# Neighbourhood attention: two pairs of score banks, one bank each for the results and the turned pieces

## The chip, the cores and the metric

One core of a Trainium2 chip runs the whole program. The metric is device time in microseconds, the median of three runs.

## The reference

Two transformer blocks over 1024 tokens of width 1024, in fp32. The change lies in one part of the first block, the neighbourhood attention: 16 heads of width 32, on a grid of 16 rows by 64 columns. A query sees the 8 grid rows around its own (`WIN_R`) and 16 columns (`WIN_C`):

```python
sc = jnp.einsum('bjqhd,bjkhd->bhjqk', qb, kg).astype(jnp.float32) * scale + bias
pr = jax.nn.softmax(sc, axis=-1).astype(vg.dtype)
o = jnp.einsum('bhjqk,bjkhd->bjqhd', pr, vg)
```

## The kernel before, in words

`neighbourhood_phase` (L2385) takes the 16 heads as four quads of four, and in each quad the 16 grid rows: 64 steps g. A step works on one grid row, 64 queries by 4 heads, against 8 rows of keys (512). It goes through these pieces of work, each a small function written once for its engine, with semaphores between them and the order written out by hand:

- `score` (PE, L2458): six matmuls in three passes (q and k are split into a high and a low part) into `psS`, two banks of 512.
- `add_bias` (DVE, L2584): for each of the two banks one instruction that adds the bias and keeps the running minimum of the negated scores. It takes no semaphore of its own, so the waits stand on the instruction before it: `clear_spare` (L2592), a memset of one column of a spare tile, or, from g = 2 on, the reciprocal in `out_of`.
- `exps` (ACT, L2553): the exponentials, one instruction for each of the two banks.
- `turn_e` (PE, L2486): eight transposes of the exponentials into `psT` (banks 4 and 5). `take` (ACT, L2562) copies them out.
- `multiply` (PE, L2496): 16 small matmuls with v into `psO` and 16 with ones into `psR`, the row sums.
- `out_of` (DVE, L2596): reciprocal of the sums, then the product into `att_T`.

Beside this, the next quad's q and k are brought into shape during the current quad: eight pieces (four of k, then four of q), one per step from r = 4 (`TURN_AT`) to r = 11. `turn` (PE, L2474) transposes a piece, `take_high` (ACT, L2540) rounds it to the high part a step later, and `take_low` (DVE, L2607) subtracts to the low part and so sets the bank free (`lowered`). The first quad's eight pieces are turned ahead of the loop.

PE's order in step g (L2527 to L2535) is turn_e(g), score(g+2), multiply(g-1), then a piece where there is one. ACT's (L2571 to L2577) is exps(g+1), take(g), then the high part of a piece. DVE's (L2636 to L2650):

```python
if g + 2 < STEPS:
    dve.wait_ge(scored, g + 3)
    dve.wait_ge(exped, 2 * g + 2)
...
if g >= 2:
    out_of(g - 2)
if g + 2 < STEPS:
    add_bias(g + 2)
if q + 1 < QUADS and 0 <= r - TURN_AT - 1 < PIECES:
    take_low(q + 1, r - TURN_AT - 1)
```

The eight banks of PSUM before: 0 and 1 the scores (one pair, so score(g) waits at L2463 until add_bias(g-1) is done), 2 and 3 the turned pieces by turns (a piece waits at L2481 for the one two back), 4 and 5 the turned exponentials, 6 and 7 results and sums by turns (multiply waits at L2501 for the out_of two back). SP loads q, k, bias and v a quad ahead (L2436 to L2448), each behind a wait on the quad that used the buffer. POOL sets the ones and does nothing else in the loop.

Of the kernel before, what the change touches and what calls it, by code (L numbers as in the profile page):

```python
# [2384 lines left out]
def neighbourhood_phase(nc, k, proj, att, after):  # L2385
    Q0, K0, V0 = 3 * 512, 4 * 512, 5 * 512
    QC = 4 * DB_H
    with ExitStack() as stack:
# [14 lines left out]
        inv_T = s.sb("inv_T", [P, GRID])  # L2403
        own = s.sb("own", [P, 2])
        neg_max = [[s.sb(f"neg_max{a}{b}", [P, 1]) for b in range(2)] for a in range(2)]
        spare = s.sb("spare", [P, 4])
        psS = [k.ps[:, b, :] for b in range(2)]
        psT = k.ps[:, 4:6, :].rearrange("p b n -> p (b n)")
        psO, psR = ([k.ps[:, 6 + a, i * GRID:(i + 1) * GRID] for a in range(2)] for i in range(2))
        psP = [k.ps[:, 2 + a, 0:PC] for a in range(2)]  # L2410

        loaded, v_loaded, bias_loaded = s.sems("loaded", 2), s.sems("v_loaded", 2), s.sems("bias_loaded", 2)
        spared, lowered, own_set, turned, taken = (s.sem(n) for n in ("spared", "lowered", "own_set", "turned", "taken"))
# [42 lines left out]
        @block.tensor  # L2456
        def _(pe):
            def score(g):  # L2458

                q, r = divmod(g, ROWS)  # L2460
                a = r % 2
                if g >= 1:
                    pe.wait_ge(biased, 2 * g)  # L2463
                if r == 0:
                    pe.wait_ge(lowered, PIECES * (q + 1))
                for i_pass, (qq, kk) in enumerate(((q_hi, k_hi), (q_lo, k_hi), (q_hi, k_lo))):
                    for b in range(2):
                        two = slice(b * 2 * DB_H, (b + 1) * 2 * DB_H)
                        last = pe.matmul(psS[b], qq[q % 2][two, r, :, :].rearrange("p h c -> p (h c)"),
                                         kk[q % 2][two, first_row(r) * GRID:first_row(r) * GRID + CH],  # L2470
                                         start=(i_pass == 0), stop=(i_pass == 2))
                last.then_inc(scored, 1)

            def turn(q, j):  # L2474
                i, m = 1 - j // (PIECES // 2), j % (PIECES // 2)
                if m == 0 and isinstance(q, int) and q == 0:
                    pe.wait_ge(k.na_loaded[i], 16)
                elif m == 0:
                    pe.wait_ge(loaded[i], 16 * q)
                if PIECES * q + j > 1:  # L2480
                    pe.wait_ge(lowered, PIECES * q + j - 1)  # L2481
                for n in range(2):
                    last = pe.transpose(psP[j % 2][:, n * P:(n + 1) * P], raw[i][:, 2 * m + n, :], k.ident[:])
                last.then_inc(turned, 1)

            def turn_e(g):  # L2486

                pe.wait_ge(exped, 2 * g + 2)
                if g >= 1:
                    pe.wait_ge(eT_ready, g)  # L2490
                for b in range(2):
                    for n in range(4):
                        last = pe.transpose(psT[:, b * CH + n * P:b * CH + (n + 1) * P], e[g % 2][b][:, n * P:(n + 1) * P], k.ident[:])
                last.then_inc(e_turned, 1)

            def multiply(g):  # L2496

                q, r = divmod(g, ROWS)
                a = r % 2
                if g >= 2:  # L2500
                    pe.wait_ge(row_out, g - 1)  # L2501
                if r == 0:
                    pe.wait_ge(v_loaded[q % 2], 32 * (q // 2 + 1))
                pe.wait_ge(eT_ready, g + 1)

                def weights(h, n):
                    at = h // 2 * CH + n * P + h % 2 * GRID
                    return eT[a][:, at:at + GRID]

                for n in range(4):  # L2510
                    row = first_row(r) + 2 * n
                    vv = (v_even if row % 2 == 0 else v_odd)[q % 2]
                    for h in range(4):
                        part = slice(h * DB_H, (h + 1) * DB_H)
                        pe.matmul(psO[a][part, :], vv[:, row // 2, part], weights(h, n), start=(n == 0), stop=(n == 3))
                for n in range(4):
                    for h in range(4):
                        part = slice(h * DB_H, (h + 1) * DB_H)
                        last = pe.matmul(psR[a][part, :], ones[:], weights(h, n), start=(n == 0), stop=(n == 3))
                last.then_inc(multiplied, 1)  # L2520

            for j in range(PIECES):
                turn(0, j)
            score(0)
            score(1)
            pe.wait_ge(ones_set, 1)
            for g in range(STEPS):  # L2527
                q, r = divmod(g, ROWS)
                turn_e(g)
                if g + 2 < STEPS:  # L2530
                    score(g + 2)
                if g >= 1:
                    multiply(g - 1)
                if q + 1 < QUADS and 0 <= r - TURN_AT < PIECES:
                    turn(q + 1, r - TURN_AT)  # L2535
            multiply(STEPS - 1)

        @block.scalar
        def _(act):
            def take_high(q, j):  # L2540
                i, m = 1 - j // (PIECES // 2), j % (PIECES // 2)
                act.wait_ge(turned, PIECES * q + j + 1)
                if i == 0 and q == 0 and m == 0:
                    act.wait_ge(own_set, 8)
                if i == 1:
                    act.copy(k_hi[q % 2][:, m * PC:(m + 1) * PC], psP[j % 2]).then_inc(taken, 1)
                    return
                for slot in range(2):
                    last = act.activation(q_hi[q % 2][:, m * PR:(m + 1) * PR, slot, :], psP[j % 2].rearrange("p (r c) -> p r c", c=GRID),
                                          ACT.Copy, scale=own[:, slot:slot + 1])  # L2550
                last.then_inc(taken, 1)

# [27 lines left out]
        def _(dve):  # L2580
# [3 lines left out]
            def add_bias(g):  # L2584

                a, off_g = g % 2, off(g % ROWS)
                for b in range(2):
                    nb = bias[g // ROWS % 2][:, b, off_g:off_g + WIN_R, :].rearrange("p r c -> p (r c)")
                    dve.tensor_tensor_reduce(sc[a][b][:], psS[b], nb, 1.0, BIG, ALU.add, ALU.min,  # L2589
                                             neg_max[a][b][:]).then_inc(biased, 1)  # L2590

            def clear_spare(col):  # L2592

                dve.memset(spare[:, col:col + 1], 0.0).then_inc(spared, 1)

            def out_of(g):  # L2596

                q, r = divmod(g, ROWS)
                dve.wait_ge(multiplied, g + 1)
                if g > 0:  # L2600
                    dve.wait_ge(row_out, g)
                dve.reciprocal(inv_T[:], psR[g % 2]).then_inc(inverted, 1)
                dve.wait_ge(inverted, g + 1)
                dve.tensor_tensor(k.att_T[:, q, r * GRID:(r + 1) * GRID], psO[g % 2], inv_T[:],
                                  ALU.mult).then_inc(row_out, 1)

            def take_low(q, j):  # L2607
                i, m = 1 - j // (PIECES // 2), j % (PIECES // 2)
                dve.wait_ge(taken, PIECES * q + j + 1)
                if i == 0 and q == 0 and m == 0:  # L2610
                    dve.wait_ge(own_set, 8)
                if i == 1:
                    cols = slice(m * PC, (m + 1) * PC)
                    dve.tensor_tensor(k_lo[q % 2][:, cols], psP[j % 2], k_hi[q % 2][:, cols].bitcast(F), ALU.subtract).then_inc(lowered, 1)
                    return
                for slot in range(2):
                    rows = slice(m * PR, (m + 1) * PR)
                    last = dve.scalar_tensor_tensor(out=q_lo[q % 2][:, rows, slot, :], in0=psP[j % 2].rearrange("p (r c) -> p r c", c=GRID),
                                                    scalar=own[:, slot:slot + 1], in1=q_hi[q % 2][:, rows, slot, :].bitcast(F),
                                                    op0=ALU.mult, op1=ALU.subtract)  # L2620
                last.then_inc(lowered, 1)
# [13 lines left out]
            add_bias(1)  # L2635
            for g in range(STEPS):  # L2636
                q, r = divmod(g, ROWS)
                if g + 2 < STEPS:
                    dve.wait_ge(scored, g + 3)
                    dve.wait_ge(exped, 2 * g + 2)  # L2640
                    if r == ROWS - 2:
                        dve.wait_ge(bias_loaded[(q + 1) % 2], 16 * ((q + 1) // 2 + 1))
                if g < 2:
                    clear_spare(2 + g)
                if g >= 2:
                    out_of(g - 2)
                if g + 2 < STEPS:
                    add_bias(g + 2)
                if q + 1 < QUADS and 0 <= r - TURN_AT - 1 < PIECES:
                    take_low(q + 1, r - TURN_AT - 1)  # L2650
# [702 lines left out]
```

## Time and profile before

| what | value |
|---|---|
| median of three runs | 3104.11 us (3103.66 to 3104.99) |
| the profiled execution | 3107.22 us |
| its span, first to last instruction | 3105.5 us |
| PE busy, weight loads busy | 2787.9 us (90%), 2190.9 us (71%) |
| DVE, ACT, POOL busy | 1740.6 (56%), 1239.4 (40%), 298.6 us (10%) |
| mean granted clock of TensorE | 0.949 of full speed |

The shares are of the whole span, and stages with other limits stand side by side in them. PE is TensorE's matmuls, PEld its weight loads, DVE VectorE, ACT ScalarE, POOL GpSimd, SP the engine that issues most transfers. A granted clock of 1.00 is 2.4 GHz, 0.50 is 1.2 GHz. Profiled executions have a time of their own, a little above the median of the runs.

### The profile page before, as it was taken

How to read it: one execution, taken by the hardware profiler on the slowest of the kernel's cores; microseconds unless marked ns; L12 is line 12 of the kernel's file. 1: busy time of each engine (PE TensorE's matmuls, PEld its weight loads, DVE VectorE, ACT ScalarE, POOL GpSimd, SP SyncE). 2: the span in 40 equal slices, each digit the busy share in tenths (PEclk: the TensorE clock that was granted, in tenths of full speed). 3: DMA queues.
4: the chain of work that ended last, by engine and by line, in shares of the span. 5: the costliest groups of instructions: out<-in, count | busy, mean ns of one | idle time of the engine just before them, and what ended most of it. 6: DMA issues, size and time to landing. Idle time of an engine off the chain costs nothing. (4 is left out here: it accounts for less than half of the span.)

```text
span 3105.5 us, 60538 instructions
## 1 busy us (share of the span) xinstructions
PE 2787.9 (90%) x24014; PEld 2190.9 (71%) x24014; DVE 1740.6 (56%) x3213; ACT 1239.4 (40%) x2039; POOL 298.6 (10%) x459
## 2 busy tenths in 40 slices
PE   7999896999869999999788999978888999968888
PEld 6787664777648877777576888765567888865557
DVE  4762777676151222222265677469865667559874
ACT  4332564785041010000065322258842332249861
POOL 0000562000031222222100000000000000000000
PEclk9999998999989999999899999989889999989989
DMA  5222755212369999999864233351035223270024
GB/s 181 91 78 76 235 164 157 76 49 78 115 263 323 374 380 380 377 374 378 286 239 152 68 109 109 123 165 28 1 123 173 78 84 110 78 219 28 14 82 142
DMA packets 226424, 509.35 MB, mean 164 GB/s; under 512 B 29217, under 2 KB 101729, under 8 KB 201537
## 3 DMA queue, kind: packets, MB, share of 16 engines
q1 hardware_dynamic: 202448, 448.57, 40.4%
q0 software_dynamic: 22640, 58.01, 6.9%
q8 instruction: 122, 2.00, 0.3%
q14 instruction: 62, 0.50, 0.1%
q10 hardware_dynamic: 1152, 0.27, 0.0%
HBM read 414.04 MB, written 93.66 MB: 163 GB/s over the span
## 5 line engine op out<-in xcount | busy, mean ns | idle before, releaser
L1933 PE MATMUL ps<-w_up,ex_xT 128*32 128x384 f32 x3072 | 343.8, 489 | 17.9 <-DMA w_up<-in_w_dram 17.0
L1935 PE MATMUL ps<-w_up,ex_xT 128*32 128x128 f32 x3072 | 348.0, 274 | 0.0
L1935 PEld LDWEIGHTS ps<-w_up,ex_xT 128*32 128x32 f32 x3072 | 331.3, 110 | 0.4
L1884 DVE TENSOR_TENSOR ex_hid<-ps,ex_act 32x128 f32<-32x128 f32 x96 | 28.2, 294 | 303.4 <-PE ps L1935 302.6
L927 ACT CAST next_w<-early 128x512 fp32r<-128x512 f32 x128 | 79.7, 622 | 256.6 <-PE ps L1245 219.4
L1960 PE MATMUL ps<-w_down,ex_hT 128*32 128x512 f32 (+1 forms) x1536 | 173.4, 491 | 6.8 <-DMA w_down<-in_w_dram 6.0
L1962 PE MATMUL ps<-w_down,ex_hT 128*32 128x256 f32 x768 | 173.6, 383 | 0.0
L1029 DVE TENSOR_TENSOR next_w<-early,next_w 128x512 fp32r<-128x512 f32 x128 | 88.2, 690 | 134.8 <-ACT next_w L927 133.9
L694 PE MATMUL ps<-mix_in_wh,mix_in_xh 128*128 128x512 f32 x384 | 152.6, 397 | 7.2 <-DVE mix_in_xl L474 3.7
L695 PE MATMUL ps<-mix_in_wl,mix_in_xh 128*128 128x512 f32 x384 | 150.7, 392 | 0.0
L696 PE MATMUL ps<-mix_in_wh,mix_in_xl 128*128 128x512 f32 x384 | 150.6, 392 | 0.0
L1933 PEld LDWEIGHTS ps<-w_up,ex_xT 128*32 128x32 f32 x3072 | 119.7, 110 | 28.6 <-DMA w_up<-in_w_dram 24.2
L1893 DVE COPY ex_y<-ps 32x256 f32<-32x256 f32 x96 | 41.0, 427 | 171.8 <-PE ps L1962 160.5
L298 POOL DMA_DIRECT2D x<-y x12 | 6.5, 538 | 1273.2 <-PE ps L674 1273.2
L3036 PE MATMUL ps<-stick_w,stick_v 128*64 128x512 f32 (+3 forms) x384 | 91.3, 558 | 38.9 <-DVE gT L3163 36.0
L1245 PE MATMUL ps<-next_w,in_sl 128*128 128x512 f32 x288 | 112.0, 389 | 0.0
L1244 PE MATMUL ps<-next_w,in_sh 128*128 128x512 f32 x288 | 112.0, 389 | 0.0
L1243 PE MATMUL ps<-next_w,in_sh 128*128 128x512 f32 x288 | 112.0, 389 | 0.0
L1846 ACT COPY ex_xT<-ps 128x768 f32<-128x768 f32 x33 | 26.3, 798 | 197.3 <-PE ps L1914 197.3
L2560 ACT ACTIVATE na_e<-na_sc,na_neg_max 128x512 f32<-128x512 f32 x128 | 85.6, 716 | 48.8 <-DVE na_neg_max L2589 48.6
L3140 DVE TENSOR_TENSOR stick_soft<-stick_z,stick_soft 128x256 f32<-128x256 f32 (+2 forms) x96 | 91.7, 955 | 21.5 <-ACT stick_soft L3083 20.9
L1243 PE MATMUL ps<-next_w,next_x 128*128 128x512 f32 x256 | 102.9, 402 | 0.0
(505 smaller groups left out, 7379.2 us busy)
## 6 DMA issues: line engine op xcount, KB each, us to landing
w_up<-in_w_dram SPq DMA_DIRECT2D x128, 1024.0 KB, 15.4
w_down<-in_w_dram SPq DMA_DIRECT2D x64, 1024.0 KB, 15.6
proj<-in_st SPq DMA_DIRECT2D x104, 256.0 KB, 2.1
da_w_ada<-in_w_ada_dram SPq DMA_DIRECT2D x32, 768.0 KB, 4.5
in_right<-in_w_in_dram SPq DMA_DIRECT2D x16, 1024.0 KB, 5.8
early<-in_w_in_dram SPq DMA_DIRECT2D x14, 1024.0 KB, 6.1
x<-proj SPq DMA_DIRECT2D x24, 512.0 KB, 5.8
proj<-mix_in_out SPq DMA_DIRECT2D x40, 256.0 KB, 2.0
```

The costliest lines, as they stand in the source:

```text
L694: pe.matmul(o, xh[:, kt, tok], wb[0], start=(kt == 0), stop=False)
L695: pe.matmul(o, xh[:, kt, tok], wb[1], start=False, stop=False)
L696: last = pe.matmul(o, xl[:, kt, tok], wb[0], start=False, stop=(kt == KT - 1))
L1243: pe.matmul(o, h[:, j, cols], wh[:, n % RING, :], start=first, stop=False, skip_group_check=n >= PLAIN)
L1244: pe.matmul(o, h[:, j, cols], wl[:, n % RING, :], start=False, stop=False, skip_group_check=n >= PLAIN)
L1245: return pe.matmul(o, l[:, j, cols], wh[:, n % RING, :], start=False, stop=end, skip_group_check=n >= PLAIN)
L1933: pe.matmul(o[group(g), :], tokens[g], wh[j][:, q, 0:HM], start=first, stop=end)
L1935: last = pe.matmul(o[BR:P, g * HQ:(g + 1) * HQ], tokens[g], wh[j][:, q, HM:], start=first and g == 0, stop=end, skip_group_check=True)
L1960: pe.matmul(psY[group(g), cols], hT[:, q, group(g)], wy[j][:, i, cols], start=first, stop=end)
L1962: last = pe.matmul(psY[BR:P, g * YQ:(g + 1) * YQ], hT[:, q, group(g)], wy[j][:, i, YM:], start=first and g != 1, stop=end, skip_group_chec ...
L3036: end = pe.matmul(psO[a * DS:(a + 1) * DS, cols(n)], v[:, s, ch:ch + DS], w[n % 2][:, a, cols(n)], start=first(n), stop=last(n), skip_grou ...
L3140: dve.tensor_tensor(ap, z[n % ZB][:, :, cols(n)], ap, ALU.max).then_inc(softed, 1)
```

## The change

Banks 0 to 3 become two pairs for the scores, used by turns; results and sums have bank 6 alone, and the turned pieces bank 7 alone (in the first quad, ahead of the loop, banks 7 and 3 by turns). The waits follow: `score` waits for the add two steps back, `turn` for the piece just before, `multiply` for the out_of just before. On DVE, `out_of` moves ahead of the waits for scores and exponentials, which now stand on a memset in every step. Uses of `psS`, `psP`, `psO` and `psR` are renamed accordingly, and `spare` gets a column for each step.

```diff
-        psS = [k.ps[:, b, :] for b in range(2)]
+        psS = [[k.ps[:, 2 * a + b, :] for b in range(2)] for a in range(2)]
...
-        psO, psR = ([k.ps[:, 6 + a, i * GRID:(i + 1) * GRID] for a in range(2)] for i in range(2))
-        psP = [k.ps[:, 2 + a, 0:PC] for a in range(2)]
+        psO, psR = (k.ps[:, 6, i * GRID:(i + 1) * GRID] for i in range(2))
+
+        def piece_bank(q, j):
+            return k.ps[:, 3 if q == 0 and j % 2 else 7, 0:PC]
...
-                if g >= 1:
-                    pe.wait_ge(biased, 2 * g)
+                if g >= 2:
+                    pe.wait_ge(biased, 2 * (g - 1))
...
-                if PIECES * q + j > 1:
-                    pe.wait_ge(lowered, PIECES * q + j - 1)
+                if q > 0:
+                    pe.wait_ge(lowered, PIECES * q + j)
+                elif j > 1:
+                    pe.wait_ge(lowered, j - 1)
...
-                if g >= 2:
-                    pe.wait_ge(row_out, g - 1)
+                if g >= 1:
+                    pe.wait_ge(row_out, g)
...
                 q, r = divmod(g, ROWS)
+                if g >= 2:
+                    out_of(g - 2)
                 if g + 2 < STEPS:
                     dve.wait_ge(scored, g + 3)
                     dve.wait_ge(exped, 2 * g + 2)
                     if r == ROWS - 2:
                         dve.wait_ge(bias_loaded[(q + 1) % 2], 16 * ((q + 1) // 2 + 1))
-                if g < 2:
-                    clear_spare(2 + g)
-                if g >= 2:
-                    out_of(g - 2)
-                if g + 2 < STEPS:
+                    clear_spare(g + 2)
                     add_bias(g + 2)
```

## Rows read from the trace of the kernel before

**Rows 1.** Windows: busy us of PE, PEld, DVE, ACT, POOL; granted clock; DMA

```profile
554.30:742.60 188.30, 183.88 (x4782) 141.97 (x4780) 133.40 (x396) 144.88 (x214) 0.00 (x0) 1.00 0.13 38
...
602.39:605.49 3.10, 3.02 (x78) 2.29 (x79) 2.00 (x6) 2.24 (x4) 0.00 (x0) 1.00 0.00 0
611.82:614.98 3.16, 3.16 (x81) 2.50 (x80) 2.33 (x8) 2.50 (x6) 0.00 (x0) 1.00 0.00 0
```

**Rows 2.** Waits of the phase, 536 to 743 us: total, times, longest

```profile
DVE na_inv_T L2602 <- PE ps L2469: 53.0, 60, 1.6
...
PEld ps L2469 <- DVE na_neg_max L2589: 17.4, 60, 2.3
```

**Rows 3.** Timeline of a plain row; in brackets the idle before and its releaser

```profile
601.04 0.68 DVE L2589 CUSTOM_DVE_ANT_0 na_sc<-ps,na_bias 128x512 f32<-128x512 f32 x1
...
602.25 0.08 DVE L2589 DVE_READ_ACCUMULATOR2_ANT na_neg_max<- 128x1 f32 x1
...
602.39 0.19 PEld L2469 LDWEIGHTS ps<-na_k_hi,na_q_hi 64*128 64x128 f32 x2 [0.32 <-DVE na_neg_max L2589]
...
603.28 0.49 PEld L2515 LDWEIGHTS ps<-na_eT,na_v_even 128*32 128x32 f32 x32 [0.36 <-issue]
...
603.40 0.56 DVE L2602 RECIPROCAL na_inv_T<-ps 128x64 f32<-128x64 f32 x1 [1.06 <-PE ps L2469]
...
603.99 0.22 DVE L2604 TENSOR_TENSOR att_T<-ps,na_inv_T 128x64 f32<-128x64 f32 x1
```

**Rows 4.** Timeline near the start, scores that wait for nothing

```profile
545.76 0.19 PEld L2469 LDWEIGHTS ps<-na_k_hi,na_q_hi 64*128 64x128 f32 x2 [0.56 <-DVE na_neg_max L2589]
...
546.79 0.69 DVE L2589 CUSTOM_DVE_ANT_0 na_sc<-ps,na_bias 128x512 f32<-128x512 f32 x1 [1.08 <-issue]
...
548.72 0.19 PEld L2469 LDWEIGHTS ps<-na_k_hi,na_q_hi 64*128 64x128 f32 x2 [0.17 <-issue]
```

**Rows 5.** Timeline of rows in which a piece is turned

```profile
610.39 0.68 DVE L2589 CUSTOM_DVE_ANT_0 na_sc<-ps,na_bias 128x512 f32<-128x512 f32 x1
610.58 0.20 PEld L2483 LDWEIGHTS ps<-ident,x 128*128 128x128 f32 x2
...
611.61 0.08 DVE L2589 DVE_READ_ACCUMULATOR2_ANT na_neg_max<- 128x1 f32 x1
611.61 0.42 DVE L2614 TENSOR_TENSOR na_k_lo<-ps,na_k_hi 128x256 fp32r<-128x256 f32 x1
...
611.82 0.18 PEld L2469 LDWEIGHTS ps<-na_k_hi,na_q_hi 64*128 64x128 f32 x2 [0.17 <-DVE na_neg_max L2589]
...
624.26 0.87 DVE L2618 SCALAR_TENSOR_TENSOR na_q_lo<-ps,na_own,na_q_hi 128x256 fp32r<-128x256 f32 x2
...
624.47 0.19 PEld L2469 LDWEIGHTS ps<-na_k_hi,na_q_hi 64*128 64x128 f32 x2 [0.17 <-DVE na_neg_max L2589]
```

**Rows 6.** Timeline of the first scores, at the lower clock

```profile
536.35 0.29 PEld L2469 LDWEIGHTS ps<-na_k_hi,na_q_hi 64*128 64x128 f32 x2 [2.24 <-DVE na_q_lo L2618]
...
538.14 0.06 DVE L2594 MEMSET na_spare<- 128x1 f32 x1 [1.85 <-PE ps L2469]
...
539.56 0.29 PEld L2469 LDWEIGHTS ps<-na_k_hi,na_q_hi 64*128 64x128 f32 x2 [2.28 <-DVE na_neg_max L2589]
```

**Rows 7.** Timeline of the last rows

```profile
740.63 0.56 DVE L2602 RECIPROCAL na_inv_T<-ps 128x64 f32<-128x64 f32 x1 [2.13 <-PE ps L2519]
740.69 0.52 PEld L2515 LDWEIGHTS ps<-na_eT,na_v_even 128*32 128x32 f32 x32 [0.29 <-issue]
```

**Rows 8.** PE's timeline and windows (as rows 1) of other stages

```profile
2170.68 0.44 PE L3036 MATMUL ps<-stick_w,stick_v 128*64 128x128 f32 x4 [2.47 <-DVE gT L3163]
...
2813.95 0.66 PE L2981 MATMUL ps<-ident,stick_raw 128*128 128x128 f32 x4 [1.06 <-DVE stick_k_lo L3127]
...
2170.70:2176.00 5.30, 5.30 (x30) 3.54 (x30) 4.99 (x9) 3.88 (x8) 0.00 (x0) 0.68 0.00 0
...
2800.00:2825.00 25.00, 20.30 (x110) 12.10 (x110) 23.74 (x29) 22.32 (x31) 0.00 (x0) 1.00 0.00 1
```

More of the change, by code:

```diff
@@ L2405, in neighbourhood_phase @@
         neg_max = [[s.sb(f"neg_max{a}{b}", [P, 1]) for b in range(2)] for a in range(2)]
-        spare = s.sb("spare", [P, 4])
-        psS = [k.ps[:, b, :] for b in range(2)]
+        spare = s.sb("spare", [P, STEPS])
+        psS = [[k.ps[:, 2 * a + b, :] for b in range(2)] for a in range(2)]
         psT = k.ps[:, 4:6, :].rearrange("p b n -> p (b n)")
-        psO, psR = ([k.ps[:, 6 + a, i * GRID:(i + 1) * GRID] for a in range(2)] for i in range(2))
-        psP = [k.ps[:, 2 + a, 0:PC] for a in range(2)]
+        psO, psR = (k.ps[:, 6, i * GRID:(i + 1) * GRID] for i in range(2))
+        def piece_bank(q, j):
+            return k.ps[:, 3 if q == 0 and j % 2 else 7, 0:PC]
         loaded, v_loaded, bias_loaded = s.sems("loaded", 2), s.sems("v_loaded", 2), s.sems("bias_loaded", 2)
@@ L2468, in score @@
                         two = slice(b * 2 * DB_H, (b + 1) * 2 * DB_H)
-                        last = pe.matmul(psS[b], qq[q % 2][two, r, :, :].rearrange("p h c -> p (h c)"),
+                        last = pe.matmul(psS[a][b], qq[q % 2][two, r, :, :].rearrange("p h c -> p (h c)"),
                                          kk[q % 2][two, first_row(r) * GRID:first_row(r) * GRID + CH],
@@ L2479, in turn @@
                     pe.wait_ge(loaded[i], 16 * q)
-                if PIECES * q + j > 1:
-                    pe.wait_ge(lowered, PIECES * q + j - 1)
+                if q > 0:
+                    pe.wait_ge(lowered, PIECES * q + j)
+                elif j > 1:
+                    pe.wait_ge(lowered, j - 1)
                 for n in range(2):
-                    last = pe.transpose(psP[j % 2][:, n * P:(n + 1) * P], raw[i][:, 2 * m + n, :], k.ident[:])
+                    last = pe.transpose(piece_bank(q, j)[:, n * P:(n + 1) * P], raw[i][:, 2 * m + n, :], k.ident[:])
                 last.then_inc(turned, 1)
@@ L2514, in multiply @@
                         part = slice(h * DB_H, (h + 1) * DB_H)
-                        pe.matmul(psO[a][part, :], vv[:, row // 2, part], weights(h, n), start=(n == 0), stop=(n == 3))
+                        pe.matmul(psO[part, :], vv[:, row // 2, part], weights(h, n), start=(n == 0), stop=(n == 3))
                 for n in range(4):
@@ L2518, in multiply @@
                         part = slice(h * DB_H, (h + 1) * DB_H)
-                        last = pe.matmul(psR[a][part, :], ones[:], weights(h, n), start=(n == 0), stop=(n == 3))
+                        last = pe.matmul(psR[part, :], ones[:], weights(h, n), start=(n == 0), stop=(n == 3))
                 last.then_inc(multiplied, 1)
@@ L2545, in take_high @@
                 if i == 1:
-                    act.copy(k_hi[q % 2][:, m * PC:(m + 1) * PC], psP[j % 2]).then_inc(taken, 1)
+                    act.copy(k_hi[q % 2][:, m * PC:(m + 1) * PC], piece_bank(q, j)).then_inc(taken, 1)
                     return
                 for slot in range(2):
-                    last = act.activation(q_hi[q % 2][:, m * PR:(m + 1) * PR, slot, :], psP[j % 2].rearrange("p (r c) -> p r c", c=GRID),
+                    last = act.activation(q_hi[q % 2][:, m * PR:(m + 1) * PR, slot, :], piece_bank(q, j).rearrange("p (r c) -> p r c", c=GRID),
                                           ACT.Copy, scale=own[:, slot:slot + 1])
@@ L2588, in add_bias @@
                     nb = bias[g // ROWS % 2][:, b, off_g:off_g + WIN_R, :].rearrange("p r c -> p (r c)")
-                    dve.tensor_tensor_reduce(sc[a][b][:], psS[b], nb, 1.0, BIG, ALU.add, ALU.min,
+                    dve.tensor_tensor_reduce(sc[a][b][:], psS[a][b], nb, 1.0, BIG, ALU.add, ALU.min,
                                              neg_max[a][b][:]).then_inc(biased, 1)
@@ L2601, in out_of @@
                     dve.wait_ge(row_out, g)
-                dve.reciprocal(inv_T[:], psR[g % 2]).then_inc(inverted, 1)
+                dve.reciprocal(inv_T[:], psR).then_inc(inverted, 1)
                 dve.wait_ge(inverted, g + 1)
-                dve.tensor_tensor(k.att_T[:, q, r * GRID:(r + 1) * GRID], psO[g % 2], inv_T[:],
+                dve.tensor_tensor(k.att_T[:, q, r * GRID:(r + 1) * GRID], psO, inv_T[:],
                                   ALU.mult).then_inc(row_out, 1)
@@ L2613, in take_low @@
                     cols = slice(m * PC, (m + 1) * PC)
-                    dve.tensor_tensor(k_lo[q % 2][:, cols], psP[j % 2], k_hi[q % 2][:, cols].bitcast(F), ALU.subtract).then_inc(lowered, 1)
+                    dve.tensor_tensor(k_lo[q % 2][:, cols], piece_bank(q, j), k_hi[q % 2][:, cols].bitcast(F), ALU.subtract).then_inc(lowered, 1)
                     return
@@ L2617, in take_low @@
                     rows = slice(m * PR, (m + 1) * PR)
-                    last = dve.scalar_tensor_tensor(out=q_lo[q % 2][:, rows, slot, :], in0=psP[j % 2].rearrange("p (r c) -> p r c", c=GRID),
+                    last = dve.scalar_tensor_tensor(out=q_lo[q % 2][:, rows, slot, :], in0=piece_bank(q, j).rearrange("p (r c) -> p r c", c=GRID),
                                                     scalar=own[:, slot:slot + 1], in1=q_hi[q % 2][:, rows, slot, :].bitcast(F),
```

## The prediction

> **What bounds the kernel now.** I read three views, in this order. The busy time of the engines, cut at the starts of two scores [rows 1], says which engine is full. The change lies in the neighbourhood phase alone; the stretch from 554.30 us, where the loop has settled, to the end of the phase at 742.60 us is 188.30 us long, PE is busy for 183.88 us of it at a granted clock of 1.00, which is 2.4 GHz, and the DMA share is 0.13, so no transfer sets the pace. One plain row takes 3.10 us with PE busy 3.02, DVE 2.00 and ACT 2.24; a row in which a piece of the next quad is turned takes 3.16 us with PE busy 3.16. The waits of the phase [rows 2] then name the loop: in 60 of the 64 rows the weight load of the scores waits for DVE's running minimum, 17.4 us in all, and in 60 rows DVE's reciprocal waits for the scores. The timeline of a plain row [rows 3] shows the order. The scores start at 602.39; DVE starts the reciprocal at 603.40, 1.01 us later, and the product at 603.99; the add of the bias takes from 601.04 to 602.33 (602.25 and the 0.08 us of the last readout), and the next scores start 0.06 us after it. So DVE and PE hand one pair of banks to and fro: 1.01 to the reciprocal, 1.29 of add and 0.06 back are 2.36 us, and the 0.74 left of 3.10 are reciprocal and product, up to the start of the next add.
>
> How much of that is slack of PE? The load ahead of the scores stood idle for 0.32 us [rows 3]; but where the scores had nothing left to wait for, the idle is still 0.17 us and is marked "issue" [rows 4]. From scores to scores that free row took 548.72 - 545.76 = 2.96 us. In rows with a piece the idle is 0.17 us as well [rows 5]: there PE is already at its own pace.
>
> **The change part by part.** *Scores in two pairs.* The wait at L2463 now asks for the row two back, whose bias add must be done before the exponentials that L2488 waits for one step earlier. It is met whenever PE arrives. A plain row goes from 3.10 to 2.96 us, 0.14 us each. Between the sixth and the last scores lie 58 distances; 24 of them hold a piece (8 in each of three quads), so 34 are plain: 34 x 0.14 = 4.8 us gained. The ends are nothing (one free row is a thin sample) and the whole idle, 34 x 0.32 = 10.9 us; I take the free row, since it is the same code without the wait.
>
> *Turned pieces in one bank.* This is the part that costs. Before, turn j waited for the piece two back, which DVE had taken a row earlier. Now (L2481) it waits for the piece just before it. PE's pass is turn of the exponentials, scores, multiply, piece; DVE's pass is results, add of the bias for those same scores, then the low part of piece j-1 (L2650). So the piece's transpose waits until DVE has waited for this pass's scores, added two biases and taken the piece, and behind it in PE's order stand the next transposes of the exponentials, the next scores and the next multiply. The new loop from scores to scores is: scores to DVE's first add 1.05 us (1.03 in the free row with its memset [rows 4], 1.01 to the reciprocal plus 0.06 for the memset [rows 3, 6]); first add to the piece's low part 611.61 - 610.39 = 1.22; the low part 0.42 for a piece of the keys, 0.87 for a piece of the queries; 0.06 to PE; piece to next scores 611.82 - 610.58 = 1.24 [rows 5]. That is 3.99 us with a piece of the keys and 4.44 with one of the queries, against 3.163 before (624.47 - 611.82 over four rows). ACT is no later: its high parts follow a copy that starts when the transposes end, and it is busy for 2.50 us of such a row [rows 1]. The first piece of a quad waits for the quad before, long done, and pays nothing; turns 1 to 4 wait for the keys, 5 to 7 for the queries. Over three quads: 12 x 0.83 + 9 x 1.28 = 10.0 + 11.5 = 21.5 us lost. The start of the add may lie between 1.01 and 1.07 us, and the hand-over to PE may take 0.13 us, as from the last readout's end at 611.69 to the scores at 611.82 [rows 5]: 20.7 to 23.4.
>
> *Results in one bank, and results ahead of the wait.* Multiply g now waits for the product of g-1. From the scores: 1.05 to the add, 1.22 to the reciprocal behind it, 0.59 + 0.22 to the end of the product, 0.06: 3.14 us. PE comes to that multiply one row and 603.28 - 602.39 = 0.89 us after those scores, at 3.85 [rows 3]. The 0.71 us between hide it. Only after the eighth piece, which no turn follows, does DVE's 0.87 us [rows 5] come first: 4.01, 0.16 too late, once a quad, 0.5 us (0 to 1.5). On DVE the results now wait for a multiply with the adds queued behind them, but that multiply ends before the scores of those adds begin, so nobody waits longer. Taking the results ahead of the wait gives DVE some 0.74 us of the path back, which is what makes the new loop no longer than written above; the memset that carries the waits, 0.06 us [rows 6] in 60 more rows, is inside the 1.05. By the Trainium skill, "Perfetto Trace Analysis", section Matmuls, groups of matmuls should move through different PSUM banks so that one is emptied under the next; one bank for the results goes against it. Taken at its word the whole 0.87 us of reciprocal, product and hand-over would stand bare in the 42 rows without a stall, 37 us, and the sum would be 54 us instead of 17. The trace speaks against that here, since transposes and scores of another bank lie between two multiplies.
>
> *The ends.* At the start, scores 1 waited 2.28 us for the first add [rows 6]; now they follow at once, at the lower clock. I take half, 1.1 us (0 to 2.3), because the first exponentials, not the scores, hold up what follows. At the end the last multiply started at 740.69, 0.06 us after the reciprocal of the row before [rows 7]; it now waits for that row's product, 0.81 us more (0 to 0.9). SP's loads wait for pieces, biases and multiplies of a quad earlier and POOL issues nothing here, so no queue gets a new wait.
>
> *The sum* is 21.5 - 4.8 + 0.5 - 1.1 + 0.8 = 16.9 us. The profiled execution took 3107.22 us with a span of 3105.5, and would be 3124.1; the median of the runs, 3104.11, lies 3.1 us lower, so I forecast 3104.1 + 16.9 = 3121.0 us. With all ends good the sum is 20.7 - 10.9 + 0 - 2.3 + 0 = 7.5 us, with all bad 23.4 + 1.5 + 0.9 = 25.8.
>
> **The rivals.** *The piece is not late* (the other side). If DVE had the earlier piece out of the bank before PE's turn, the 21 stalls would be gone and the pairs would show alone: -4.8 - 1.1 + 0.8 = -5.1, 3099 us; with the whole idle of 0.32 us, -11.2, 3093 us. It decides from the point where a stall costs less than 0.25 us (5.1 over 21), or 0.53 with the larger gain. For it: DVE is busy for only 2.33 of 3.16 us in such a row [rows 1]. Against it: in DVE's program the piece stands behind an add that needs this pass's scores, and PE cannot issue the next pass ahead of its turn. Chance 0.08, of it 0.05 for 3099 and 0.03 for 3093.
>
> *The clock falls in the stalled rows.* PE would stand for 0.8 to 1.3 us in each of seven rows running. In another stage a gap of 1.06 us was followed by no fall, the granted clock staying 1.00 over the 25 us around it, while after a gap of 2.47 us it was 0.68 over the next 5.3 us, so the lower level of 1.2 GHz in most of that time [rows 8]. If it fell, the path from scores to add would be 538.14 - 536.35 = 1.79 us instead of 1.05 [rows 6], and the transposes would grow by about as much: some 1.4 us a row, 13 us for the nine rows with queries, 29 for all 21: 3134 to 3150 us. Chance 0.08. The Trainium skill names such a case, "TensorE: Matmul & The Clock Gate", section on psum-queue depth-cycling: short idle spells between groups at each turn of the banks made the clock go to and fro. Of this trace the gap of 2.47 us agrees and the one of 1.06 us does not.
>
> *Multiply waits for the product in every row.* It decides where DVE's path is 0.71 us longer than worked out; at the worst, all of 0.87 us bare in 42 rows, 37 us, it is 3158 us. Chance 0.04.
>
> **How the numbers follow.** The forecast has the remaining 0.80. All of its bounds, 7.5 to 25.8 us above 3104.1, give 3112 to 3130, which is the range; it leaves out the rivals, 2 in 10. A measurement of this kernel can tell about 0.2%, 6.2 us, from no change: 3098 to 3110 is "same". Faster is 0.03, same 0.05, slower 0.80 + 0.08 + 0.04 = 0.92.
>
> **What would show it.** In the profile of the changed kernel: the wait of the scores for DVE's minimum gone from the list, and in its place the load of the piece's transpose (L2483's successor) waiting for DVE's low parts, 21 times, some 0.8 and 1.3 us above its row; plain rows of 2.96 us; seven rows running of 3.99 and then 4.44 us in each of the first three quads, and none in the last; the phase longer by 17 us and all other stages as long as now. It is wrong if the piece's transpose has no wait, if plain rows stay at 3.10, if the granted clock in the stalled rows is below 1.00, or if multiply waits for the product in plain rows.

## The result, and the profile after

The changed kernel takes 3123.35 us (median of five runs, 3120.30 to 3128.15), the kernel before in the same comparison 3104.99 us: the ratio is 1.0058, with a 95% interval of 1.0047 to 1.0069. That is 18 us (14.6 to 21.4) slower. The profiled execution, the fastest of the five, took 3120.30 us. From the page:

```profile
span 3118.5 us, 60599 instructions
...
PE 2779.5 (89%) x24014; PEld 2186.3 (70%) x24014; DVE 1743.6 (56%) x3273; ACT 1243.5 (40%) x2039; POOL 298.1 (10%) x459
```

All of the loss that a trace can place is in the neighbourhood phase. From the first transpose of a piece to the end of the last product it took 215.44 us before (527.26 to 742.70) and takes 230.16 us now (527.41 to 757.57), 14.7 us more; the rest of the span is 2888.3 us against 2890.1. The waits in the phase (total, times, longest), which answer to [rows 2]:

```profile
PEld ps L2488 <- DVE na_q_lo L2623: 12.0, 9, 1.3
...
PEld ps L2472 <- issue: 10.4, 62, 0.2
...
PEld ps L2488 <- DVE na_k_lo L2619: 7.9, 9, 0.9
...
PEld ps L2520 <- DVE att_T L2609: 2.8, 6, 1.1
```

The scores' load (now L2472) waits for nothing that another engine does, 62 times 0.17 us. In its place the load of a piece's transpose (L2488) waits for DVE's low parts: 9 times for the queries here, 9 for the keys, and 3 more of the keys that the profile puts under "issue", its name for an idle to which it finds no releaser: the 21 of the code. The timeline of one such row, to be held against [rows 5]:

```profile
561.26 0.18 PEld L2472 LDWEIGHTS ps<-na_k_hi,na_q_hi 64*128 64x128 f32 x2 [0.17 <-issue]
...
562.28 0.69 DVE L2594 CUSTOM_DVE_ANT_0 na_sc<-ps,na_bias 128x512 f32<-128x512 f32 x1 [1.59 <-issue]
...
563.50 0.42 DVE L2619 TENSOR_TENSOR na_k_lo<-ps,na_k_hi 128x256 fp32r<-128x256 f32 x1
...
563.97 0.20 PEld L2488 LDWEIGHTS ps<-ident,x 128*128 128x128 f32 x2 [0.88 <-DVE na_k_lo L2619]
...
565.21 0.19 PEld L2472 LDWEIGHTS ps<-na_k_hi,na_q_hi 64*128 64x128 f32 x2 [0.17 <-issue]
```

Read it downwards: scores at 561.26, DVE's first add 1.02 us later, the low part 1.22 us after that, its end at 563.92, the piece 0.05 us on, the next scores 1.24 us after the piece. Before, the piece at 610.58 stood ahead of the low part at 611.61; now it stands behind one. The windows from scores to scores, columns as in [rows 1], give the stalled rows and a plain one:

```profile
554.30:757.57 203.27, 181.94 (x4772) 141.05 (x4772) 131.71 (x448) 146.94 (x213) 0.00 (x0) 1.00 0.12 36
...
557.31:561.26 3.95, 3.23 (x81) 2.49 (x80) 2.33 (x8) 2.62 (x4) 0.00 (x0) 1.00 0.03 6
577.59:582.00 4.41, 3.24 (x81) 2.50 (x81) 2.78 (x9) 3.03 (x5) 0.00 (x0) 1.00 0.02 4
595.29:598.25 2.96, 2.96 (x80) 2.28 (x80) 2.00 (x8) 2.26 (x4) 0.00 (x0) 1.00 0.15 60
```

PE has the same 3.2 us of work in a row with a piece as before, in 3.95 us with a piece of the keys and 4.41 with one of the queries; in the plain row it is busy throughout. The granted clock is 1.00 over the whole stretch.

### The profile page after: what moved, and what is told of

Same layout as the page of the kernel before. It is cut to its first block and busy times, and to the rows that moved or that the text cites. A ratio compares the mean times of both kernels' runs of the same rounds, so it can differ in the third digit from the quotient of the medians.

```text
span 3118.5 us, 60599 instructions
## 1 busy us (share of the span) xinstructions
PE 2779.5 (89%) x24014; PEld 2186.3 (70%) x24014; DVE 1743.6 (56%) x3273; ACT 1243.5 (40%) x2039; POOL 298.1 (10%) x459
## 5 line engine op out<-in xcount | busy, mean ns | idle before, releaser
L2594 DVE CUSTOM_DVE_ANT_0 na_sc<-ps,na_bias 128x512 f32<-128x512 f32 x128 | 83.0, 686 | 70.4 <-issue 40.6
```

## The experiments

Six kernels, and the change profiled again. Times of the first four stand against 21 runs of the kernel before on the same chip (median 3104.25 us), of the next two against 14 (3105.94 us). "Phase" is measured as above.

**The order alone.** The kernel before, with the one edit on DVE (and a wider spare tile):

```diff
+                if g >= 2:
+                    out_of(g - 2)
                 if g + 2 < STEPS:
                     dve.wait_ge(scored, g + 3)
                     dve.wait_ge(exped, 2 * g + 2)
...
-                if g < 2:
-                    clear_spare(2 + g)
-                if g >= 2:
-                    out_of(g - 2)
-                if g + 2 < STEPS:
+                    clear_spare(g + 2)
                     add_bias(g + 2)
```

> The kernel before, with nothing changed but DVE's order: reciprocal and product ahead of the wait for scores, a memset carrying that wait; banks and PE's waits as before. Theory (the order alone frees the plain rows): from scores to DVE's add 1.05 us, 1.29 us of adds and 0.06 us back are 2.40 us, under PE's own 2.95, so plain rows go from 3.10 to 2.95 us, rows with a piece stay at 3.16, no piece waits; 34 rows by 0.15 us are 5 us: about 3100 us, ratio 0.998. Rival (the second pair of score banks is what frees PE): plain rows stay at 3.10 us and the time at 3105 us.

Measured: 3101.74 us, ratio 0.9987 (0.9978 to 0.9996), phase 209.75 us. The timeline of a plain row:

```profile
595.00 0.19 PEld L2469 LDWEIGHTS ps<-na_k_hi,na_q_hi 64*128 64x128 f32 x2 [0.17 <-issue]
...
596.02 0.69 DVE L2589 CUSTOM_DVE_ANT_0 na_sc<-ps,na_bias 128x512 f32<-128x512 f32 x1 [0.91 <-ACT na_e L2560]
...
597.24 0.55 DVE L2602 RECIPROCAL na_inv_T<-ps 128x64 f32<-128x64 f32 x1
...
597.95 0.19 PEld L2469 LDWEIGHTS ps<-na_k_hi,na_q_hi 64*128 64x128 f32 x2 [0.17 <-issue]
```

The adds are done by 597.32, the reciprocal runs behind them, and the scores start at 597.95, 2.95 us after the last, with the idle of 0.17 us that a free load shows too. One pair of banks is enough: the second add's read of the bank ends 0.6 us before PE writes it again. The theory holds and the rival falls. By the ratio this kernel is some 4 us (1 to 7) faster than the kernel before, and its phase is 5.7 us shorter: 2.95 us for 3.10 in each plain row, and 8.46 us for 9.13 from the last scores to the last product.

**The second pair taken back.** The changed kernel, with

```diff
-        psS = [[k.ps[:, 2 * a + b, :] for b in range(2)] for a in range(2)]
+        psS = [[k.ps[:, b, :] for b in range(2)] for a in range(2)]
...
-                if g >= 2:
-                    pe.wait_ge(biased, 2 * (g - 1))
+                if g >= 1:
+                    pe.wait_ge(biased, 2 * g)
```

> The changed kernel with the second pair of score banks taken back: one pair in banks 0 and 1, scores wait for the add of the row before; results in one bank, pieces in one bank and the new order stay. Theory (the pair is worth nothing once the results stand ahead of the wait): rows as in the changed kernel, 2.95 us plain, 3.95 and 4.40 us where a piece waits, and about 1 us more at the start; the time of the changed kernel, 3123 us. Rival (the pair frees the plain rows): plain rows of 3.10 us, 5 us more: 3128 us.

Measured: 3122.45 us, ratio 1.0057 (1.0043 to 1.0070), phase 232.09 us, 1.9 over the change. Of that, 1.4 us lie between the first and the seventh scores (19.03 us for 17.63), the rest in single rows some 0.1 to 0.3 us longer. Its timeline, a plain row and a stalled one:

```profile
598.64 0.19 PEld L2472 LDWEIGHTS ps<-na_k_hi,na_q_hi 64*128 64x128 f32 x2 [0.17 <-issue]
...
601.59 0.19 PEld L2472 LDWEIGHTS ps<-na_k_hi,na_q_hi 64*128 64x128 f32 x2 [0.17 <-issue]
...
617.63 0.19 PEld L2472 LDWEIGHTS ps<-na_k_hi,na_q_hi 64*128 64x128 f32 x2 [0.17 <-issue]
...
619.86 0.42 DVE L2619 TENSOR_TENSOR na_k_lo<-ps,na_k_hi 128x256 fp32r<-128x256 f32 x1
620.34 0.20 PEld L2488 LDWEIGHTS ps<-ident,x 128*128 128x128 f32 x2 [0.88 <-DVE na_k_lo L2619]
...
621.58 0.18 PEld L2472 LDWEIGHTS ps<-na_k_hi,na_q_hi 64*128 64x128 f32 x2 [0.17 <-issue]
```

Plain rows are 2.95 us and the stalled row 3.95 us without the second pair. So the pair gives nothing in the loop and shortens the start: by 1.4 us against this profile of the change, and by 0.5 and 0.8 against its two further ones, which took 18.55 and 18.28 us between the same scores. The timed runs of the two kernels do not differ.

**Pieces taken early.** The changed kernel; ACT's `take_high` moves to the head of its step, DVE's `take_low` ahead of the wait for scores:

```diff
                 if g >= 2:
                     out_of(g - 2)
+                if q + 1 < QUADS and 0 <= r - TURN_AT - 1 < PIECES:
+                    take_low(q + 1, r - TURN_AT - 1)
                 if g + 2 < STEPS:
...
                     add_bias(g + 2)
-                if q + 1 < QUADS and 0 <= r - TURN_AT - 1 < PIECES:
-                    take_low(q + 1, r - TURN_AT - 1)
```

> The changed kernel with the taking of a piece moved up: ACT's high part at the start of its step, DVE's low part ahead of the wait for scores; all banks as in the change. Theory (the stall is the piece being taken behind the adds of the same step): the waits of the piece's transposes for the low parts go, the seven rows of 3.95 and 4.40 us become 3.16, with one or two near 3.4 where ACT's longer order holds up the transposes; the phase loses 18 to 20 us: 3101 to 3105 us. Rival (one bank for the pieces costs by itself, whatever the order): the rows stay at 3.95 and 4.40 us, 3123 us.

Measured: 3102.05 us, ratio 0.9993 (0.9984 to 1.0002), phase 211.49 us, 18.7 us less than the change. Its timeline with a piece of the queries:

```profile
626.57 0.19 PEld L2472 LDWEIGHTS ps<-na_k_hi,na_q_hi 64*128 64x128 f32 x2 [0.17 <-issue]
...
626.68 0.88 DVE L2623 SCALAR_TENSOR_TENSOR na_q_lo<-ps,na_own,na_q_hi 128x256 fp32r<-128x256 f32 x2 [0.23 <-ACT na_q_hi L2554]
...
627.58 0.69 DVE L2594 CUSTOM_DVE_ANT_0 na_sc<-ps,na_bias 128x512 f32<-128x512 f32 x1
...
628.49 0.20 PEld L2488 LDWEIGHTS ps<-ident,x 128*128 128x128 f32 x2
...
628.88 0.86 PEld L2498 LDWEIGHTS ps<-ident,na_e 128*128 128x128 f32 x8 [0.19 <-issue]
...
629.90 0.18 PEld L2472 LDWEIGHTS ps<-na_k_hi,na_q_hi 64*128 64x128 f32 x2 [0.17 <-issue]
```

The low part ends at 627.56, before the piece at 628.49, which waits for nothing. Rows are 3.16 us, and two of each quad 3.34: there the transposes of the exponentials start 0.19 us later than PE could, and by the program what they wait for is ACT, whose order got longer. With the same single bank the stall is gone, so it was the place of the taking in the orders of DVE and ACT, not the bank.

**The pairs with the old order.** The changed kernel with the lines of the order put back as they were.

> The changed kernel with DVE's old order: results behind the wait for scores, all banks and PE's waits as in the change. Theory (one bank for the results is free only because they come ahead of the wait): multiply waits for a product that starts 1.01 us after this step's scores and needs 0.87 us more, so it starts 1.88 us after them and not 0.89: plain rows of 3.95 us, rows with a waiting piece of 4.7 and 5.1 us; some 53 us more than the changed kernel, 3176 us. Rival (with two pairs of score banks the order does not matter): 3123 us.

Measured: 3172.64 us (one run), phase 285.00 us, 54.8 over the change. A row with a piece, in its timeline:

```profile
660.57 0.18 PEld L2472 LDWEIGHTS ps<-na_k_hi,na_q_hi 64*128 64x128 f32 x2 [0.17 <-issue]
...
661.58 0.56 DVE L2607 RECIPROCAL na_inv_T<-ps 128x64 f32<-128x64 f32 x1 [2.31 <-PE ps L2472]
...
662.45 0.49 PEld L2520 LDWEIGHTS ps<-na_eT,na_v_even 128*32 128x32 f32 x32 [1.36 <-DVE att_T L2609]
```

Multiply starts 1.88 us after the scores, to the hundredth as expected, since its bank is free only when the product is done. Plain rows are 3.93 us, stalled ones 4.67 and 5.13, but for two with queries, from 584.35 us on, which take 5.80 and 5.81 us at a mean granted clock of 0.88 and 0.83. The single result bank costs next to nothing only under the new order.

**One bank for the results, by itself.** The order alone, with `psO` and `psR` in bank 6 and `multiply` waiting for the out_of just before:

```diff
-        psO, psR = ([k.ps[:, 6 + a, i * GRID:(i + 1) * GRID] for a in range(2)] for i in range(2))
+        psO, psR = ([k.ps[:, 6, i * GRID:(i + 1) * GRID] for a in range(2)] for i in range(2))
...
-                if g >= 2:
-                    pe.wait_ge(row_out, g - 1)
+                if g >= 1:
+                    pe.wait_ge(row_out, g)
```

> The kernel with the new order alone, and results and sums in one bank, so that each multiply waits for the product of the row before; one pair of score banks and two banks for the pieces stay. Theory (one bank for the results costs next to nothing when they stand ahead of the wait for scores): plain rows stay at 2.95 and rows with a piece at 3.16 us, the row after each quad's last piece is some 0.1 us longer, the last multiply starts 0.8 us later: 1 us over the order alone, 3101 to 3104 us. Rival (a single bank leaves the 0.87 us of reciprocal, product and hand-over bare in each row): plain rows of 3.8 us, 3150 us.

Measured: 3101.30 us, ratio 0.9984 (0.9975 to 0.9993), phase 210.66 us, 0.9 over the order alone. The timeline:

```profile
591.05 0.19 PEld L2469 LDWEIGHTS ps<-na_k_hi,na_q_hi 64*128 64x128 f32 x2 [0.17 <-issue]
...
593.29 0.55 DVE L2602 RECIPROCAL na_inv_T<-ps 128x64 f32<-128x64 f32 x1
...
593.87 0.23 DVE L2604 TENSOR_TENSOR att_T<-ps,na_inv_T 128x64 f32<-128x64 f32 x1
...
594.00 0.18 PEld L2469 LDWEIGHTS ps<-na_k_hi,na_q_hi 64*128 64x128 f32 x2 [0.17 <-issue]
...
594.90 0.49 PEld L2515 LDWEIGHTS ps<-na_eT,na_v_even 128*32 128x32 f32 x32 [0.37 <-issue]
```

The product ends at 594.10 and the multiply that needs the bank comes at 594.90, 0.8 us later: hidden. The row after a quad's last piece is 2.99 us instead of 2.95. The rest of the cost stands at the end, where nothing hides it: from the last scores to the last product it takes 9.24 us instead of 8.46.

**One bank for the pieces, by itself.** The kernel before, with the pieces in one bank and the wait of the change:

```diff
-                if PIECES * q + j > 1:
-                    pe.wait_ge(lowered, PIECES * q + j - 1)
+                if q > 0:
+                    pe.wait_ge(lowered, PIECES * q + j)
+                elif j > 1:
+                    pe.wait_ge(lowered, j - 1)
```

> The kernel before with nothing changed but the turned pieces in one bank, each waiting for the one just before it; DVE's old order, one pair of score banks, two banks for results. Theory (the stalled row is the path from scores through DVE to the piece and back; in the old order the results lie on it too): 1.01 + 0.74 + 1.22 + 0.42 + 0.06 + 1.24 = 4.69 us with a piece of the keys and 5.14 with one of the queries, seven rows in each of three quads, plain rows of 3.10: 12 x 1.53 + 9 x 1.98 = 36 us more than before, 3140 us. Rival (a stall is worth the same with either order): 3.95 and 4.40 us, 21 us more, 3125 us.

Measured: 3143.96 us (one run), 38.0 us over the kernel before, phase 254.70 us. Rows are 4.67 and 5.12 us where 4.69 and 5.14 were expected, so the results in the path cost 0.72 us a stalled row, and the new order, which takes them out, saves that too. But four of the nine rows with queries are longer, 5.51 to 5.87 us. Windows of an ordinary one and of the longest, and PE's timeline of both:

```profile
639.67:644.80 5.13, 3.24 (x82) 2.50 (x81) 2.79 (x8) 3.09 (x5) 0.00 (x0) 1.00 0.00 0
702.24:708.11 5.87, 3.98 (x82) 3.08 (x81) 2.79 (x8) 3.09 (x5) 0.00 (x0) 0.87 0.00 0
```

```profile
643.56 0.44 PE L2487 MATMUL ps<-ident,x 128*128 128x128 f32 x2 [1.89 <-DVE na_q_lo L2622]
...
706.13 0.44 PE L2487 MATMUL ps<-ident,x 128*128 128x128 f32 x2 [1.89 <-DVE na_q_lo L2622]
```

PE stood for 1.89 us in both, and the mean granted clock is 1.00 in the one and 0.87 in the other: part of that ran at 1.2 GHz. In the change, where PE's idle in such a row is 1.17 us, the clock stayed.

**The change profiled again.**

> The changed kernel once more, profiled again to see where its executions differ from each other (its five runs lay between 3120 and 3128 us, and the profiled one was the fastest). Theory (the spread is outside the phase, in the other stages' clock): the phase again 230 us long, all rows with a waiting piece at 3.95 to 4.02 and 4.40 us, granted clock 1.00 in them. Rival (in some executions the clock falls in the stalled rows): single rows of 5 us and more among them, the granted clock under 1.00 there, the phase 232 us and longer.

> A further profile of the changed kernel, for the same question. Theory (spread outside the phase): phase of 230 us, no row over 4.45 us after the clock has risen at the start. Rival (clock falls in the stalled rows in some executions): rows of 5 us and more, phase of 232 us and longer.

Measured, on another chip, where one run of the kernel before took 3100.87 us: 3120.10 and 3121.09 us, phases 231.17 and 230.73 us. In both every row with a waiting piece is 3.95 to 4.02 or 4.40 to 4.41 us, as in the first profile, so in three profiles the clock did not fall there. The executions of 3126 and 3128 us have no trace; whether their phase was longer stays open.

## Why the prediction was right, point by point

The direction and the size were right: 3121.0 was forecast and 3123.35 measured, within the range of 3112 to 3130. That the median came within 2.4 us is in part luck: the forecast set it 3.1 us below the profiled execution, as it was in the kernel before, and here it lies 3.05 us above, while the profiled execution itself, forecast at 3124.1, took 3120.30. So it is not shown that profiled executions run a little above the median. The terms, from the profile:

- *The waiting pieces.* Forecast 3.99 and 4.44 us a row, 21.5 us in all; seven rows took 586.40 - 557.31 = 29.09 us in the first quad, 29.08 and 29.07 in the others, against 7 x 3.163 = 22.14: 20.8 us. Taking the pieces early made the phase 18.7 us shorter, which shows the cause.
- *The plain rows.* 2.95 us for a forecast of 2.96: 34 x 0.15 = 5.1 us gained, 4.8 forecast. The size was right, **the reason was not**: the step that failed is the one that gave this gain to the scores in two pairs. With one pair and the new order the rows are as short; the gain belongs to the reciprocal and product having left the path from scores to scores. The prediction named that move, and booked nothing for it in plain rows; the term came out because both moves were in the change. The sum of the path without the results, 1.05 + 1.29 + 0.06 = 2.40 us, lies under PE's 2.95 and could have been written down from [rows 3, 4, 6].
- *One bank for the results.* Forecast 0.5 us and hidden otherwise; by itself it cost 0.9 us over the whole phase: 0.04 us in each of the three rows after a quad's last piece, where 0.16 was forecast, and 0.8 us at the end, the next term. The 37 us that the rule of the Trainium skill ("Perfetto Trace Analysis", section Matmuls) would have made of it did not come, since the multiply finds its bank empty 0.8 us ahead; under the old order, where it does not, the same bank made plain rows 3.93 us.
- *The ends.* The start gained 1.3 us in this profile (first piece to sixth scores, 25.06 to 23.79), 1.1 forecast, but in the two further ones it took 24.69 and 24.42 us, a gain of 0.4 and 0.6. The clock has a share in that: the second scores to the third took 4.04 us at a mean granted clock of 0.77 in this profile, and 4.91 us at 0.50 in each of the others. The end was forecast to lose 0.8 and lost 0.1 (last scores to the last product, 9.13 to 9.23). The last multiply did wait for the product:

```profile
755.59 0.49 PEld L2520 LDWEIGHTS ps<-na_eT,na_v_even 128*32 128x32 f32 x32 [1.10 <-DVE att_T L2609]
```

  but the last transposes began 4.18 us after the last scores instead of 4.86. That is the new order's doing: alone it brings the end to 8.46 us, and one bank for the results on top of it to 9.24. So the bank did cost the 0.8 us forecast, and the prediction had not counted the 0.7 that the order gives here.
- *The rivals.* The piece was late in every one of the 21 rows. The clock did not fall in the stalled rows of any of the three profiles; that it did in both kernels that have one bank for the pieces and the old order shows that the rival had its ground. Such a row was 0.4 to 0.8 us longer there, not the 1.4 of the forecast.

The terms add up to 20.8 - 5.1 + 0.1 - 1.3 + 0.1 = 14.6 us, the 14.7 by which the phase grew. The timed runs say 18, with an interval that begins at 14.6; no term of the phase is left for the 3 us between, and it was not found elsewhere. The rest of the span, which no edit touches, lies between 2885.9 and 2891.0 us in the ten profiles, so a difference of 3 us cannot be placed in it; where they come from stays open.

## What to carry to other kernels

A second buffer pays only where the path from write to free is longer than the engine's own row: write that path out in both orders first, for moving one step out of it can do what the second buffer was to do, and here 5.7 us of the phase came from an order and at most 2 from the second pair of banks. Where a buffer is cut to one, look in the reader's program at what stands ahead of the read: the copy of the turned piece behind two adds cost 0.8 to 1.3 us each time, and with the copy ahead of them the same bank cost 0.2 us in two rows of each quad.

## What was not expected of the hardware

Stalls of nearly 2 us in a loop that repeats every 5.1 us let the granted clock fall in some rows and not in others: 0.87 over the row from 702.24, 1.00 over the one from 639.67, with the same 1.89 us of idle in each. In the pairs with the old order it fell in two rows although PE's idle was split there, 0.92 us ahead of the multiply and 0.91 ahead of the piece; in the change one gap of 1.17 us a row left it at 1.00 in three profiles. And ACT's copy of the turned exponentials, of the same shape in all kernels, has a median of 0.991 us before, 0.992 with one bank for the pieces alone, and 1.013 to 1.015 in the six others; it is not on the path, and no run looked for why.
